# The end of a decoder layer: last down unit by columns, last sums begun and counted in PSUM, bias from one-row products, four stores

## What is computed

```
t = x * (1 + scale2) + shift2
y = 0
for e in range(16):
    hid = silu(t @ w_gate[e]) * (t @ w_up[e])
    y = y + combine[:, e:e + 1] * (hid @ w_down[e])
x = alpha * x + gate2 * y
out = (x - mean(x)) * rsqrt(var(x) + eps) * ln2_g + ln2_b
```

## Time and profile before

| | |
|---|---|
| median of three runs | 1773.83 us (1769.34 to 1775.88) |
| the profiled execution, first to last instruction | 1768.5 us |
| PE busy | 1509.3 us, 85% |
| DVE / ACT / POOL busy | 589.0 / 182.6 / 361.6 us |
| weights queue of SP | 623.15 MB, 85.1% of 16 engines' span |
| last half unit in place, PE starts on it | 1743.05 us |
| last instruction of DVE ends | 1761.93 us |

### The profile page before, as it was taken

The page is one execution under the profiler, slowest core; times in us unless marked ns, Lnnn a source line. Parts: engine busy times, 40 slices in busy tenths (PEclk is TensorE's granted clock), DMA queues, the critical chain, the costliest instruction groups (busy, mean ns, idle before and its releaser), DMA issues.

```text
span 1768.5 us, 27368 instructions
## 1 busy us (share of the span) xinstructions
PE 1509.3 (85%) x11924; PEld 1002.6 (57%) x11924; DVE 589.0 (33%) x1079; ACT 182.6 (10%) x442; POOL 361.6 (20%) x161
## 2 busy tenths in 40 slices
PE   7799999999999999986799966798976557898556
PEld 6578888888888878653444522433434224335222
DVE  0453657877676243431111211112020110222014
ACT  0001013101010100141100100100101001001001
POOL 0005730178677867300000000000000000000000
PEclk9899999999999999988899978898998788999888
DMA  9997896678778754549997899998999999999996
GB/s 386 424 427 218 351 393 250 250 321 370 313 310 338 285 224 174 221 171 427 426 409 282 334 427 426 425 425 347 420 427 427 425 429 426 422 411 419 428 426 248
DMA packets 51059, 630.56 MB, mean 357 GB/s; under 512 B 5775, under 2 KB 8240, under 8 KB 11848
## 3 DMA queue, kind: packets, MB, share of 16 engines
q1 hardware_dynamic: 49768, 623.15, 85.1%
q10 hardware_dynamic: 1120, 5.01, 0.7%
HBM read 624.47 MB, written 3.67 MB: 355 GB/s over the span
## 4 chain that ended last, share of the span: by engine, by line
PE 59%; DMA 32%; DVE 4%; issue 2%; POOL 1%; SPq 0%; DVEq 0%; ACT 0%; POOLq 0%
PE bank L1518 23%; PE bank L908 14%; DMA ring<-in_w_up_gate 9%; DMA ring<-in_w_down 9%; PE bank L1280 8%; PE bank L920 6%; DMA region_g<-in_w_up_gate 5%; DMA ring<-in_ada_w 4%; DMA region_g<-in_w_down 4%; PE bank L877 2%; PE bank L1356 2%; PE bank L932 2%; DVE ada_rows L2067 2%; DMA ring<-in_w_in 1%; POOL ring L762 1%
## 5 line engine op out<-in xcount | busy, mean ns | idle before, releaser
L762 POOL TENSOR_TENSOR ring<-ring 128x1024 f32<-128x1024 f32 x152 | 359.2, 2390 | 329.0 <-DMA ring<-in_w_in 224.0
L908 PE MATMUL bank<-ring,region_b 128*32 128x256 f32 (+1 forms) x3104 | 307.0, 478 | 122.9 <-DMA ring<-in_w_up_gate 96.9
L908 PEld LDWEIGHTS bank<-ring,region_b 128*32 128x32 f32 (+1 forms) x3104 | 129.5, 128 | 279.9 <-issue 141.7
L920 PE MATMUL bank<-ring,region_f 128*32 128x256 f32 (+1 forms) x1984 | 176.7, 451 | 60.8 <-DMA ring<-in_w_down 60.6
L1518 PE MATMUL bank<-ring,region_a 128*128 128x256 f32 x768 | 171.3, 380 | 0.5 <-ACT region_g L1863 0.5
L1518 PE MATMUL bank<-ring,region_x 128*128 128x256 f32 x768 | 170.4, 379 | 0.8 <-issue 0.7
L1518 PEld LDWEIGHTS bank<-ring,region_a 128*128 128x128 f32 x768 | 145.3, 190 | 23.0 <-issue 2.7
L920 PEld LDWEIGHTS bank<-ring,region_f 128*32 128x32 f32 (+1 forms) x1984 | 74.1, 122 | 146.9 <-issue 68.0
L1518 PEld LDWEIGHTS bank<-ring,region_x 128*128 128x128 f32 x768 | 145.3, 190 | 21.0 <-issue 1.1
L2555 DVE TENSOR_TENSOR work<-work,bank 128x128 f32<-128x128 f32 (+1 forms) x32 | 10.3, 321 | 424.8 <-ACT work L1771 424.8
L2067 DVE SCALAR_TENSOR_TENSOR bank<-ring,condT,bank 128x512 f32<-128x512 f32 x192 | 144.8, 754 | 5.8
(11 more groups left out here) (248 smaller groups left out, 1279.9 us busy)
## 6 DMA issues: line engine op xcount, KB each, us to landing
ring<-in_w_up_gate SPq DMA_DIRECT2D x111, 2048.0 KB, 29.3
ring<-in_w_down SPq DMA_DIRECT2D x56, 2048.0 KB, 21.9
ring<-in_ada_w SPq DMA_DIRECT2D x44, 2048.0 KB, 11.9
ring<-in_w_in SPq DMA_DIRECT2D x31, 2048.0 KB, 14.1
region_g<-in_w_up_gate SPq DMA_DIRECT2D x16, 2048.0 KB, 25.2
ring<-in_w_branch SPq DMA_DIRECT2D x8, 2048.0 KB, 14.4
ring<-in_w_out SPq DMA_DIRECT2D x8, 2048.0 KB, 10.3
region_g<-in_w_down SPq DMA_DIRECT2D x8, 2048.0 KB, 31.3
```

Source lines behind the costliest of these rows:

```text
L762: ins = pool.tensor_tensor(quarter(s, *out)[:, k:k + 4, :], quarter(s, *in0)[:, k:k + 4, :], quarter(s, *in1)[:, k:k + 4, :], op)
L908: last = nc.tensor.matmul(bank_of(x, j)[n * c:n * c + n, 0:2 * m], tokens(x, 8 * half + k), w[:, k % 4, :, m * c:m * c + m], start=(half = ...
L920: last = nc.tensor.matmul(bank_of(x, q)[n * c:n * c + n, 0:m], hidT[x][:, k, :], w[:, k % 4, m * c:m * c + m], start=(k == 0), stop=(k == ...
```

## The change

1. **Unit 5 of the last expert by columns.** The host lays its two halves out by output columns: half h holds, for all eight k, columns h*128 to h*128+127 of each of the four blocks of 256. `down_columns` makes 32 products of 128 columns for a half in place of 16 products of 256.
2. **Last sums in PSUM.** For the narrow form, PE puts the old `acc` into the bank by a product with the identity (`begun`, 512 columns, eight in all) and the scatter is added to it. DVE no longer adds: it counts the sums in PSUM with `bn_stats` of 128 columns (`stats_of_last`, 32 of them), and ACT copies them to `acc` (`take_last`, four of 512 and eight of 2x128 columns). Two `bn_aggr` work over 16 groups each. Of unit 5 each half has its own scale, scatter, count and copy.
3. **Bias by one-row products.** `ln2b` is loaded early by ACT as four rows of 512 at partitions 0, 32, 64 and 96; `beta` multiplies a row of ones with such a row, eight times, the four of a tile in different row strips. The two parts of DVE read the bias from PSUM. SP loads `ln2g` alone.
4. **Four stores** of 1024 columns, three on SP, one (tile 1, columns 0 to 1023) on ACT.

The wide form of the last expert keeps its order, with statistics behind the last addition; it is not the one that runs here. The diff, cut to what matters:

```diff
-NORM_BANKS = ((0, 1, 4, 5), SUM_BANKS)
+NORM_BANKS = ((7, 2, 3, 1), (0, 4, 5, 6))
+LAST_BANKS = (0, 4, 5, 6)
...
             sp.dma_start(ln2g, ln2_g_d.to_broadcast([P, D])).then_inc(s_ln2, 16)
-            sp.dma_start(ln2b, ln2_b_d.to_broadcast([P, D])).then_inc(s_ln2, 16)
-            for a in range(TT):
-                for q in range(4):
-                    cols = slice(q * 512, (q + 1) * 512)
-                    if q in BY_PE[a]:
-                        sp.wait_ge(tile_out, 4 * a + q + 1)
-                    else:
-                        sp.wait_ge(out_ready, q - len(BY_PE[1]) + 1)
-                    sp.dma_start(out_d[a * P:(a + 1) * P, cols], acc[:, a, cols]).then_inc(s_out, 16)
-            sp.wait_ge(s_out, 16 * 4 * TT)
+            for q in range(2):
+                sp.wait_ge(tile_out, 2 * q + 2)
+                cols = slice(q * 1024, (q + 1) * 1024)
+                sp.dma_start(out_d[0:P, cols], acc[:, 0, cols]).then_inc(s_out, 16)
+            sp.wait_ge(out_ready, 2)
+            sp.dma_start(out_d[P:T, 1024:D], acc[:, 1, 1024:D]).then_inc(s_out, 16)
+            sp.wait_ge(s_out, 16 * 4)
...
+            def down_columns(x, h):
+
+                w = expert_half(g, le * E_UNITS + 5, h).rearrange("p (k c j) -> p k c j", k=8, c=4)
+                n, own = P // strips(x), 4 // strips(x)
+                for k in range(8):
+                    for c in range(strips(x)):
+                        out = bank_of(x, 1)[n * c:n * c + n, 0:256 * own].rearrange("p (c h j) -> p h c j", c=own, h=2)
+                        last = nc.tensor.matmul(out[:, h], hidT[x][:, k, :], w[:, k, own * c:own * c + own, :],
+                                                start=(k == 0), stop=(k == 7), tile_position=(0, n * c),
+                                                skip_group_check=True)
+                return last
...
+            def begun(bank, q, c):
+
+                out = psum[bank][:, :].rearrange("p (a n) -> p a n", a=TT)
+                cols = slice(q * 1024 + c * 256, q * 1024 + (c + 1) * 256)
+                return nc.tensor.matmul(out, ident, acc[:, :, cols], start=True, stop=False, skip_group_check=True)
+
+            def beta(a, n):
+
+                return nc.tensor.matmul(psum[NORM_BANKS[a][n]][:, :], ones[32 * n:32 * n + 1, :],
+                                        ln2b_rows[32 * n:32 * n + 1, :], start=True, stop=n >= len(BY_PE[a]),
+                                        tile_position=(32 * n, 0), skip_group_check=True)
+
+            def first_sums_of_last():
+
+                pe.wait_ge(y_ready, ne * 2 + 3)
+                pe.wait_ge(extras_added, ne + 1)
+                for c in range(len(SUM_BANKS)):
+                    pe.wait_ge(m_taken[c], add_job(g, le, 0, True) + 1)
+                    begun(SUM_BANKS[c], 0, c)
...
+            def half_of_last(h):
+
+                pe.wait_ge(last_scaled, h + 1)
+                if h == 1:
+                    pe.wait_ge(last_taken, 4)
+                for a in range(TT):
+                    for c in range(4):
+                        first = a * 256 + h * P
+                        last = nc.tensor.matmul(psum[LAST_BANKS[c]][:, first:first + P],
+                                                back0[le % 2][32 * c:32 * c + 32, a, :],
+                                                ysb[1][32 * c:32 * c + 32, h * P:(h + 1) * P],
+                                                start=False, stop=True, tile_position=(32 * c, 0),
+                                                skip_group_check=True)
+                last.then_inc(last_full, 1)
+
+            def end_of_last():
+
+                first_sums_of_last()
+                for c in range(3):
+                    begun(LAST_BANKS[c], 1, c)
+                loaded_half(5, 0)
+                down(base, 1, first).then_inc(last_y, 1)
+                pe.wait_ge(m_taken[SUM_BANKS.index(LAST_BANKS[3])], add_job(g, le, 0, True) + 2)
+                begun(LAST_BANKS[3], 1, 3)
+                half_of_last(0)
+                pe.wait_ge(s_ln2b, 64)
+                for c in range(1, len(SUM_BANKS)):
+                    pe.wait_ge(m_taken[c], add_job(g, le, 0, True) + 2)
+                for n in range(3):
+                    beta(0, n)
+                loaded_half(5, 1)
+                down(base, 1, last).then_inc(last_y, 1)
+                half_of_last(1)
+                beta(0, 3)
+                pe.wait_ge(last_taken, 8)
+                for n in range(4):
+                    ins = beta(1, n)
+                ins.then_inc(beta_full, 1)
...
+            if ne == NE - 1 and base == NARROW:
+                end_of_last()
...
+            def take_last():
+
+                for c in range(len(SUM_BANKS)):
+                    act.wait_ge(first_stats, c + 1)
+                    act.activation(acc[:, :, c * 256:(c + 1) * 256],
+                                   psum[SUM_BANKS[c]][:, :].rearrange("p (a n) -> p a n", a=TT), ACT.Copy)\
+                       .then_inc(m_taken[c], 1)
+                for h in range(2):
+                    for c in range(4):
+                        act.wait_ge(last_stats, 4 * h + c + 1)
+                        first = 1024 + c * 256 + h * P
+                        both = psum[LAST_BANKS[c]][:, :].rearrange("p (a n) -> p a n", a=TT)
+                        act.activation(acc[:, :, first:first + P], both[:, :, h * P:(h + 1) * P], ACT.Copy)\
+                           .then_inc(last_taken, 1)
...
+            if ne == NE - 1:
+                act.activation(exp_table, eps[:, :], ACT.Sqrt)
+                if base == NARROW:
+                    take_last()
...
+                if name == "M1" and (kind, j, b) == ("branch", 3, 1):
+                    for n in range(4):
+                        load(ln2b_rows[32 * n:32 * n + 1, :], ln2_b_d[n:n + 1, :], s_ln2b)
...
+            act.wait_ge(tile_out, 4 + len(BY_PE[1]))
+            load(out_d[P:T, 0:1024], acc[:, 1, 0:1024], s_out)
...
+                    def stats_of_last():
+
+                        for c in range(len(SUM_BANKS)):
+                            dve.wait_ge(m_full[c], add_job(g, le, 0, True) + 1)
+                            for a in range(TT):
+                                ins = stats(a, 2 * c, psum[SUM_BANKS[c]][:, a * 256:(a + 1) * 256])
+                            ins.then_inc(first_stats, 1)
+                        for h in range(2):
+                            dve.wait_ge(last_y, h + 1)
+                            dve.tensor_tensor(ysb[1][:, h * P:(h + 1) * P], psum[1][:, h * P:(h + 1) * P],
+                                              g2n[:, 256 + h * P:256 + (h + 1) * P], ALU.mult).then_inc(last_scaled, 1)
+                            dve.wait_ge(last_full, h + 1)
+                            for c in range(4):
+                                for a in range(TT):
+                                    first = a * 256 + h * P
+                                    ins = stats(a, 8 + 4 * h + c, psum[LAST_BANKS[c]][:, first:first + P])
+                                ins.then_inc(last_stats, 1)
...
+                        for c in range(len(SUM_BANKS)):
+                            dve.wait_ge(m_taken[c], add_job(g, le, 0, True) + 2)
+                        dve.wait_ge(last_taken, 8)
...
             dve.wait_ge(centred_ready, 4 * TT)
+            dve.wait_ge(beta_full, 1)
             for q in range(len(BY_PE[1]), 4):
                 last_part = acc[:, 1, q * 512:(q + 1) * 512]
                 dve.scalar_tensor_tensor(out=last_part, in0=last_part, scalar=lrstd[:, 1:2],
-                                         in1=ln2b[:, q * 512:(q + 1) * 512], op0=ALU.mult, op1=ALU.add)\
+                                         in1=psum[NORM_BANKS[1][q]][:, :], op0=ALU.mult, op1=ALU.add)\
                    .then_inc(out_ready, 1)
```

More of the change, by code:

```diff
@@ L404, in program @@
         gcmp = small[:, 608:640]
+        end_stat = small[:, 448:640].rearrange("p (a n s) -> p a n s", a=TT, s=6)
         toe_row = region_f[0:H, 0:TOE]
@@ L518, in program @@
         x_dve = [None] + [sem(f"extra{x}_dve") for x in EXTRA]
-        out_ready = sem("second_tile_ready")
-        tile_out = sem("first_tile_ready")
+        out_ready = sem("parts_finished_by_dve")
+        beta_full = sem("beta_of_last_part_full")
+        tile_out = sem("parts_finished_by_act")
         centred_ready = sem("centred_part_ready")
@@ L950, in turn_weights, with end_of_wide @@
+            def end_of_wide():
+                pe.wait_ge(s_ln2b, 64)
+                for b in range(len(SUM_BANKS)):
+                    pe.wait_ge(m_taken[b], add_job(g, le, 1, True) + 2)
+                for a in range(TT):
+                    for n in range(4):
+                        ins = beta(a, n)
+                ins.then_inc(beta_full, 1)
             def turn_weights():
@@ L1253, in expert_pe @@
             announced = pe.mark_branch_hint_location() if base == WIDE else None
+            if ne == NE - 1 and base == NARROW:
```

(39 more changed lines are left out.)

63 lines of the change are left out of this document (38 added, 25 removed).

## The result

The kernel after takes 1783.78 us (median of six runs, 1781.43 to 1784.36), the kernel before 1772.30 in the same session (six runs). The ratio is 1.0061, 95% interval 1.0047 to 1.0075, so it is 10.8 us (8.3 to 13.3) slower. The forecast was 1771.0 with a range up to 1775.5. The profiled execution of after took 1783.64 us with a span of 1781.8, 13.3 more than the span of 1768.5 before.

The account below looks back on a forecast made before the run. Weights by DMA bound the kernel up to the last half unit; then DVE bounds sums and norm, SP's issues with the transfer the stores. 1.25 + 1.55 = 2.8 us off the median 1773.83 gives 1771.0, range 1766.0 to 1775.5.

Parts of the forecast that it names:

- Only what follows that half is open.: Expert stage: weights set the time up to the last half unit, unchanged; only the tail from 1743.05 us can move.
- five rivals: Half-clock list 0.07, one-row products not overlapping 0.15, stores not faster 0.11, last half not held up 0.05, wide form runs 0.02.
- if the weights' last landing moves: Closing sign in the profile after that the forecast is wrong; no size given.
- (a): Last half's landing to first reciprocal, 11.31 us before: additions leave DVE, PE's list becomes the bound, 1.25 us gained.
- Rival 2: PE's one-row bias products don't overlap: 1.6 us more before the last half, 1.2 before the norm, gain 0.3; chance 0.15.
- second table load: On ACT before the root: 1.28 us, would cost as much as (a) gains; only one load seen at L1771.
- The sum starts when the first scale ends: Start of PE's list in (a): first scale ends at 1735.32 + 0.42, so the sum begins at 1735.8 us.
- rival 1: PE's list, 11.6 us of work, all at half clock: end at 1777.3, 8.8 us slower; chance 0.07.
- (b): The norm, 1754.36 to 1761.93, 7.57 us before: no instruction fewer, bias from PSUM costs nothing, no gain.
- ACT's store goes out alone at 1761.9 and ends at about 1765.8, the same time: Stores, if the clock falls in the norm: its products end 1.6 us later, the end stays the same.
- (c): The stores, 1761.93 to 1768.5: four on two queues take 5.0 us for 6.57, 1.55 us gained.

Follow-up runs that it names:

- experiment 4: The changed kernel with wide forms 256 instructions later than before by jumped-over padding, plus two thrown-away PE products ahead of the norm: 1.0002 to before, 1773.36 us.
- aligned kernel: The changed kernel with jumped-over padding that puts PE's wide forms 256 instructions later than in the kernel before: 1.0014 to before, 1775.35 us.

## Why the prediction was wrong

**The failed step: "Only what follows that half is open."** The sum began at 1735.8 as if nothing before could move, because the weights' bytes and order stay. They do, but the same argument needs PE to take them on time, and PE was held at its returns from the wide forms because their code had moved: 8.3 us by making the shift of after 256, 9.0 us by giving before the shift of 200, of 10.8 in all. In this sense the change does touch what lies ahead of 1733 us. None of the five rivals covered it; the closing sentence named the symptom ("if the weights' last landing moves") without a cause or a price. The trace of before had the warning, ten waits of PE with the releaser "issue" at the gate-and-up products, the longest, 7.89 us, where the program comes back from a wide form; and the diff shows that the narrow form, which stands ahead of these bodies, grows.
The Trainium skill (Runtime: NRT & Kernel Launch, Instruction fetch mechanics) says that code is fetched in sequence in blocks of 256 instructions and that a branch taken to a block not held has to wait for its fetch. The runs agree as far as they go: PE's long waits stand where the program has jumped, and a shift of 256 costs nothing where 200 costs 9.0 us. That the place is what costs is shown; that the waits are for the fetch of code is argued from this and from the instruction transfers. It was weighed nowhere in the prediction.

**(a): the list was priced about right, its start was not.** In the pair of before and after the gain is 0.69 us in place of 1.25. The last half starts at 12.42 us from the scale's start where 12.03 was forecast, the reciprocal at 18.35 for 17.78. The terms, from start to start where one follows the other at once: eight `begun` 7.45 (forecast 6.8), three bias products 0.96 (0.95), half scatter 0.55 (0.65), second half 1.95 (1.95), statistics from PSUM 1.68 for eight (1.6), two aggregations 1.03 (0.68). The price of 0.85 us for a `begun` came from taking the 0.27 us of idle time before a row off its 5.39 us, which don't hold it; and 16 groups cost 0.5 us where the estimate added 1 ns for each element. Rival 2 is out: one-row products on different strips do overlap (its own price was added up wrong, 1.6 and 1.2 us more make a span of 1768.5 and not 1768.2). The list itself ran at full clock, and no second table load came before the root.

But the 0.69 us are luck of the pair. "The sum starts when the first scale ends" took the scale to stand at a fixed distance from the weights, and the traces together say otherwise:

| | last half landed to reciprocal, us | scale to reciprocal, us |
|---|---|---|
| order of before, seven traces | 9.79 to 11.41 (before 11.35) | 15.96 to 19.09 |
| order of after, four traces | 10.69 (after), 12.22, 12.33, 12.58 | 18.35 to 18.50 |
| five `begun` earlier, two traces | 6.94 and 6.22 | 14.22 and 13.88 |

The scale waits for PE's products of unit 4's last half. In after they ran at full clock (1745.82, 1.93 us). In the other three traces of this order they took 3.55 to 3.64 us, here that of experiment 4, where the granted clock was 0.50:

```profile
1733.97 3.64 PE L946 MATMUL bank<-ring,region_f 128*32 128x256 f32 x32 [0.78 <-DMA ring<-in_w_down]
```

Then the scale, and with it the whole list, comes 1.6 to 1.7 us later behind the weights, and so does the reciprocal. In the order of before slow products there cost nothing: a trace that has them (3.45 us, the run with DVE's and ACT's increments) has 9.79, since what follows the scale waits for the next half anyway. By the means of these few traces the new order is 1.1 us slower from the landing to the reciprocal (11.96 against 10.86), not 1.25 faster. It is rival 1's mechanism at a point where the prediction didn't look, just ahead of the list.

**(b), wrong.** The prediction saw that the clock might fall in the norm and called the price nothing, "ACT's store goes out alone at 1761.9 and ends at about 1765.8, the same time". The products didn't end 1.6 us later but 2.6 (7.99 for 5.39), and the store wasn't alone: ACT's six copies were late, so SP's second store went out at about 1774.4, its third at 1774.78 and ACT's at 1776.12, and 1.5 MB flowed together at 387 to 396 GB/s. In the aligned kernel, whose norm took 7.08 us, the repair is worth 2.1 us (the two intervals just overlap). The step worked out one store's transfer and took the others to be under way by then.

**(c), right.** 2.6 us (0.9 to 4.3) alone against 1.55, and 4.7 to 5.8 us from DVE's end with the clock held, against 5.0. The Trainium skill's rule (DMA: Bandwidth & Descriptors, Issuing engines are not separate DMA queues), by which (c) would have stayed at 6.57, is no guide here: the prediction counted 3.8 us of issue behind ready data, and the run gained 2.6.

**What doesn't close.** 1.0002 with place and clock repaired is 0.4 us above before and 3.2 above the forecast's -2.8. Of these 3.2, (a) explains some 2.3: 1.1 lost in place of 1.25 gained, as far as seven and four traces can say. The rest is within the interval of that run, 1.6 us each way; whether a little of the place is left in it (the last expert's narrow form is still 226 longer) isn't told apart. Nor is it known which return pays at which offset: 128 hit 887 us, 200 hit 1231 in all three traces and 1604 in two of them, and 320 (64 beyond the aligned place) hit 994 and 1301.

## What to carry to other kernels

When an edit changes the number of instructions of an engine, look at what stands behind it in the program: bodies that are reached by a jump may cost more in their new place, and the cost shows as idle time with no releaser, far from the edit; compare landmarks of both traces before the place of the change, and test with padding that is jumped over. Independent products of PE belong into its waits for DMA and not into the list behind the last landing, and a wait right ahead of dense products is worth filling, if late results bunch the stores behind them. A short tail should be measured from the landing that nothing in it can move, over several executions, before a term of 1 us is worked out from one trace.

## What was not expected of the hardware

- The same jump back costs PE 7.87 to 8.48 us in ten traces and 11.39 to 12.49 in the three whose code was moved by 200 instructions. At another expert it is 6.55 and 6.70 us in two of these three, against 0.77 before.
- A semaphore increment by PE's sequencer took 0.16 us in a row of 200.
- Three products of 512 columns with one row each, on three row strips, took 1.03 us together at full clock; the `begun` products of 128 rows took 0.9 us each.
- Two aggregations of 16 groups took 1.03 us, against 0.26 for one of four groups.
